# Splitting each weight block into high and low part with one instruction per engine in place of two

## The reference

```python
# first block (256 tokens)
proj = rmsnorm(x, g) @ w_in
merged = sum(sigmoid(gate_n) * (o_n @ w_branch_n) for n in range(3))
x = x + rmsnorm(merged @ w_out, g)
u = causal_depthwise_conv(rmsnorm(x, g) @ w_ffn_up, conv_w, conv_b)
x = x + rmsnorm((gelu(u_gate) * u_val) @ w_ffn_down, g)
# second block: two layers over 256 latent and 256 context tokens;
# the second layer's late part is for the latent tokens alone
m = silu(cond) @ w_mod + b_mod                      # 9 x 1024 modulation values
x = x + 0.5 * m * swiglu(modulate(rms_norm(x)), w_in, w_out)
x = x + m * mixer(attention, fourier, gates)
x = x + 0.5 * m * swiglu(...)
```

## Time and profile before

| | us |
|---|---|
| median of 3 runs (3000.58 to 3006.28) | 3004.92 |
| the profiled execution, first to last instruction | 3003.6 |
| TensorE matmul busy | 2742.5 (91%) |
| VectorE busy | 2033.8 (68%) |
| GpSimd busy | 1600.6 (53%) |
| ScalarE busy | 1054.9 (35%) |
| mean granted TensorE clock | 0.947 |

### The profile page before, as it was taken

The page is one execution under the profiler, slowest core; times in us unless marked ns, Lnnn a source line. Parts: engine busy times, 40 slices in busy tenths (PEclk is TensorE's granted clock), DMA queues, the critical chain, the costliest instruction groups (busy, mean ns, idle before and its releaser), DMA issues.

```text
span 3003.6 us, 45318 instructions
## 1 busy us (share of the span) xinstructions
PE 2742.5 (91%) x15118; PEld 2345.7 (78%) x15118; DVE 2033.8 (68%) x4077; ACT 1054.9 (35%) x1699; POOL 1600.6 (53%) x654
## 2 busy tenths in 40 slices
PE   7898878777999999988997999999999979888998
PEld 7867878776888877956786788887888868688997
DVE  4864876686887666364879888668886662656642
ACT  4344335524232132246221433214232142453542
POOL 3516836554665444335254566445665554457675
PEclk9899879987999999999998999999999989999999
DMA  5604524353443444201344344443443442035454
GB/s 175 204 22 137 172 85 140 121 153 118 154 140 118 130 143 126 64 22 57 99 126 126 112 140 135 119 137 119 147 140 111 129 138 92 22 103 164 140 169 125
DMA packets 487725, 365.71 MB, mean 122 GB/s; under 512 B 7484, under 2 KB 486286, under 8 KB 487616
## 3 DMA queue, kind: packets, MB, share of 16 engines
q1 hardware_dynamic: 485176, 359.14, 39.2%
q10 hardware_dynamic: 2440, 5.16, 0.5%
HBM read 363.19 MB, written 1.08 MB: 121 GB/s over the span
## 4 chain that ended last, share of the span: by engine, by line
PE 54%; issue 21%; POOL 12%; DVE 10%; ACT 2%; DMA 1%; POOLq 0%; DVEq 0%; SPq 0%; ACTq 0%
PE bank L1485 46%; POOL w_lo L595 12%; DVE mod_acc L1079 3%; DVE mod_acc L1075 1%; ACT work L738 1%; PE bank L1874 1%; DVE stat L1396 1%; PE bank L1495 1%; PE bank L1852 1%; PE bank L1618 1%; PE bank L1811 1%; DMA mod_raw<-in_w_mod 1%; PE bank L1861 1%; DVE root L1414 1%; PE bank L1803 0%
## 5 line engine op out<-in xcount | busy, mean ns | idle before, releaser
L595 POOL TENSOR_TENSOR w_lo<-raw,w_hi 128x1024 fp32r<-128x1024 f32 (+2 forms) x602 | 1523.5, 2546 | 1332.9 <-ACT w_hi L653 938.5
L1485 PE MATMUL bank<-u_hi,w_hi 128*128 128x512 f32 (+1 forms) x2488 | 866.8, 348 | 31.4 <-DVE work L1280 27.7
L1485 PE MATMUL bank<-u_hi,w_lo 128*128 128x512 f32 (+1 forms) x2488 | 856.9, 344 | 0.0
L1485 PE MATMUL bank<-u_lo,w_hi 128*128 128x512 f32 (+1 forms) x2488 | 856.2, 344 | 0.0
L653 ACT ACTIVATE w_hi<-raw 128x1024 fp32r<-128x1024 f32 (+3 forms) x436 | 408.9, 952 | 1080.0 <-PE bank L1485 857.5
L1079 DVE SCALAR_TENSOR_TENSOR mod_acc<-mod_raw,cond,mod_acc 128x128 f32<-128x128 f32 x2016 | 615.4, 377 | 0.0
L1485 PEld LDWEIGHTS bank<-u_hi,w_hi 128*128 128x128 f32 x2488 | 486.2, 195 | 85.5 <-DVE work L1280 29.5
L1485 PEld LDWEIGHTS bank<-u_lo,w_hi 128*128 128x128 f32 x2488 | 485.5, 195 | 52.1 <-issue 1.5
L1485 PEld LDWEIGHTS bank<-u_hi,w_lo 128*128 128x128 f32 x2488 | 484.5, 195 | 52.3
L1075 DVE TENSOR_SCALAR mod_acc<-mod_raw,cond 128x128 f32<-128x128 f32 x288 | 260.6, 944 | 117.4 <-DMA mod_raw<-in_w_mod 117.2
L1485 PE MATMUL bank<-hid_hi,w_hi 128*128 128x512 f32 (+1 forms) x880 | 314.3, 357 | 15.5 <-DVE hid_lo L1270 7.2
(11 more groups left out here) (222 smaller groups left out, 3614.5 us busy)
## 6 DMA issues: line engine op xcount, KB each, us to landing
raw<-in_ffn_w_in SPq DMA_DIRECT2D x88, 1024.0 KB, 5.1
mod_raw<-in_w_mod SPq DMA_DIRECT2D x144, 512.0 KB, 3.8
raw<-in_w_in SPq DMA_DIRECT2D x67, 1024.0 KB, 5.3
raw<-in_ffn_w_out SPq DMA_DIRECT2D x64, 704.0 KB, 4.5
raw<-in_w_ffn_up SPq DMA_DIRECT2D x22, 1024.0 KB, 5.1
raw<-in_w_ffn_down SPq DMA_DIRECT2D x16, 704.0 KB, 4.5
raw<-in_w_attn_out SPq DMA_DIRECT2D x8, 1024.0 KB, 5.0
raw<-in_w_o SPq DMA_DIRECT2D x8, 1024.0 KB, 5.0
```

Source lines behind the costliest of these rows:

```text
L595: pool.tensor_tensor(st.half(t, w_lo[slot]), st.half(t, raw[slot]), st.half(t, w_hi[slot]).bitcast(f32), ALU.subtract).then_inc(lo_ready, 1)
L1485: ins = pe.matmul(dst, s, v, start=first and n == 0, stop=final and n == 2)
```

## The change

`half` goes and `whole` takes its place. ScalarE and GpSimd issue one instruction each for the whole block. The ScalarE instruction waits for the second group of block n. `hi_ready` and `lo_ready` count blocks, so each of TensorE's waits, for the first half too, is a wait for the whole block.

```diff
-    def half(self, t, block):
-        if self.cols == P:
-            a, b = (0, DOWN_HALF) if t == 0 else (DOWN_HALF, self.kt)
-            return block[:, a * P:b * P].rearrange("p (k n) -> p k n", n=P)
-        return block[:, 0:self.kt * BLK].rearrange("p (k n) -> p k n", n=BLK)[:, :, t * P:(t + 1) * P]
+    def whole(self, block):
+        return block[:, 0:self.kt * self.cols]
...
     def parts(self, i, c, t):
-        return i * (2 * self.per) + (2 * (self.first + c) + t + 1)
+        return i * self.per + (self.first + c + 1)
...
-                    s = st.parts(i, c, 1) - 4
+                    s = st.parts(i, c, 1) - 2
...
-                    for t in range(2):
-                        pool.wait_ge(hi_ready, st.parts(i, c, t))
-                        pool.tensor_tensor(st.half(t, w_lo[slot]), st.half(t, raw[slot]), st.half(t, w_hi[slot]).bitcast(f32),
-                                           ALU.subtract).then_inc(lo_ready, 1)
+                    pool.wait_ge(hi_ready, st.parts(i, c, 1))
+                    pool.tensor_tensor(st.whole(w_lo[slot]), st.whole(raw[slot]), st.whole(w_hi[slot]).bitcast(f32),
+                                       ALU.subtract).then_inc(lo_ready, 1)
...
                 act.wait_ge(raw_ready[n % 2], i * (8 * st.per) + 16 * (n // 2 + 1))
-                for t in range(2):
-                    act.wait_ge(group_done, st.freed(i, c, t))
-                    act.activation(st.half(t, w_hi[n % 2]), st.half(t, raw[n % 2]), ACT.Copy).then_inc(hi_ready, 1)
+                act.wait_ge(group_done, st.freed(i, c, 1))
+                act.activation(st.whole(w_hi[n % 2]), st.whole(raw[n % 2]), ACT.Copy).then_inc(hi_ready, 1)
```

More of the change, by code:

```diff
@@ L634, in split @@
                 act.wait_ge(raw_ready[s % 2], 16 * (s // 2 + 1))
-                for t in range(2):
[L636 to L642, removed]
+                if s >= 2:
+                    old = [q for q in stream if q.first <= s - 2 < q.first + q.blocks][0]
+                    q = s - 2 - old.first
+                    act.wait_ge(group_done, old.freed(q // old.per, q % old.per, 1))
+                act.activation(st.whole(w_hi[s % 2]), st.whole(raw[s % 2]), ACT.Copy).then_inc(hi_ready, 1)
             def split_two_ahead(st, i, c, final):
```

## The result

The changed kernel takes 3069.15 us (median of 4 runs, 3061.49 to 3070.0), the one before 3005.6 in runs beside it: a ratio of 1.021, 95% interval 1.0194 to 1.0226. It is slower beyond doubt; whether by a full 2% the interval leaves open. The profiled execution has a span of 3066.5 us for 3003.6, so 62.9 us are to be placed. Of all executions behind this document one ran at a much lower granted clock (3153.4 us at 0.817, in experiment 11, where the others have 0.936 to 0.951), and it is left out.

A forecast was written before the change was run, and what follows sets the result against it. Wide stages were taken as bound by TensorE, up_11 as keeping TensorE busy, up1 by VectorE held by GpSimd. Terms 13 + 4 + 8 + 13 + 3 + 7 + 0 + 4 + 1 = 53 us gave 3058 us, 1.8% slower; range 3012 to 3085.

The forecast's parts named there:

- `up1`: Narrow stage: VectorE held a second time by a whole subtraction, body 17.2 us for 15.83, ten times: +13 us.
- Cost of a whole-block instruction: ScalarE's split and GpSimd's subtraction of 2048 elements take 1.90 and 4.7 us; 1408 elements take 1.37 and 3.25.
- `up_11`, the series: Narrow stage: matmuls, split and subtraction run in series, 12.8 us a round for 11.52, ten rounds: +13 us.
- `up1` opens up: Rival: TensorE's pause leaves VectorE 2.1 us in up1, no second hold, -30 for +13: 3015 us, chance 0.17.
- the state keeps itself up: Argument against a shorter up1: once VectorE is held, the later L858 pushes the split behind it.
- wide bodies: Wide stages: the series of 1.9 and 4.7 us lies under the other buffer's 10.9 us: 0.
- `gates1`: gates1_0 and gates1_1, bound by VectorE: two holds of 4.7 us replace four of 2.4: 0, within 1 us a body.
- `down_11`: Narrow stage with the load in its ring: +0.4 us for each of 8 rounds, last block later: +4 us.
- `down1`: down1, its last body bound by the ring as in down_11, and the start: together +3 us.
- Blocks of `attn_out_1` and `gates_10`: Eight narrow blocks bound as up_11 is, four rounds: +5 us.
- branches: Twelve branch blocks and four of four_out_1, bound by the load ring, plus entry of the next gemm: +7 us.
- norms: After down projections and w_o, the last subtraction ends 0.7 us later; nine places, half of them felt: +4 us.

The follow-up runs named there:

- experiment 11: Whole instructions and one step per block in gates1_0, gates1_1 and gates1_2 alone, against the kernel before: 3012.95 us, ratio 1.0028.
- Experiment 3: Kernel before with halves kept, but both halves wait for the whole block and TensorE gets one step per block, everywhere: 3030.75 us, 1.0089.
- experiment 1: Kernel before with only ScalarE's split as one instruction per block; GpSimd and TensorE keep halves: 3031.78 us, 1.0089.
- experiment 2: Kernel before with only GpSimd's subtraction as one instruction per block; ScalarE keeps halves: 3068.62 us, 1.0216.
- experiment 6: Kernel before; in up1 alone ScalarE's halves wait for the whole group, GpSimd for the whole high part, TensorE goes by halves: 3000.13 us, 0.9992.
- experiment 8: Kernel before with whole instructions and one step per block everywhere but in up1, which keeps halves: 3074.28 us, 1.0242.
- experiment 4: Kernel before with the change, one instruction each per block, in up1 alone: 2974.89 us, 0.9909.
- experiment 5: Kernel before with halves everywhere, but in up1 alone all waits are for the whole block: 2973.74 us, 0.9894.
- experiment 12: Kernel before with the change in up1 and all wide stages, halves in the narrow ones: 2983.83 us, 0.9927.

## Why the forecast came out as it did

3069 lies 11 us above the forecast and in its range, but this nearness is luck: in the traces `up1` came out 37.5 us below its term and all the rest 47.4 above theirs. By its own steps:

**Cost of a whole-block instruction: right.** ScalarE 1.91 to 1.92 us (1.90 forecast), GpSimd 4.50 to 4.65 without VectorE in its way (4.7 forecast). For 1408 elements: 1.38 and 3.19 to 3.24 (1.37 and 3.25). Some of the arithmetic was loose without moving the result: the two pieces of ScalarE's slope are 0.97 and 0.82 ns an element and not both 0.85, and the lowest bounds add up to 6.49 and not 6.45. The Trainium skill's GPSIMD Engine Reference (section "Elementwise — side-by-side cycle accounting") with its 4497 ns was nearer to the shortest, 4.50, and my line nearer to the usual 4.62.

**`up_11`, the series: right.** 12.78 us a round for 12.8 and +12.0 for +13; with the change in this stage alone +13.3. Experiment 3 shows that it is the series: +10.2 with halves.

**`up1`: wrong, in its sign too, and this is the step that failed.** The forecast put the second split of a body 8.1 to 9.6 us after the release of L858 (now L850), and so gave VectorE 0 to 1.5 us between the subtractions. The first half of the working was right: the split ends 5.3 us after that release and the subtraction 10.0 (L850 at 510.49; 515.81; 520.51). But the second split starts at 520.95, 10.46 after the release. I had taken TensorE's end from the phase that it had before, and had not let it slide with its own later start, though the sum for `up_11` did so. 0.9 us more decided between +13 and -24.5. The rival "`up1` opens up" named this mechanism, its threshold of 2.1 us and -30 us; I gave it 0.17 because "the state keeps itself up". That is right for each part alone, where the long body comes back even after a short one (experiments 1, 2 and 6), and wrong for the parts together.

**`gates_11`: not in the sum.** It has TensorE, ScalarE's sigmoid, VectorE's gate and a branch's statistics in a chain inside each block, and I had counted narrow gemms with slack in VectorE only. +14.6, by itself +12.5: one piece is the sigmoid behind a longer split, one the hold of 4.49 us for 2.36, the rest the lower clock (0.76 for 0.89) of a TensorE that now pauses. I did not separate the three. Long splits alone give +4.2, the waits alone +6.3, and long subtractions with one step for TensorE +11.2 (experiments 1, 3 and 2), so the long subtractions are probably the largest. `gates_01` has the same build: +6.4, where the forecast had 0 for wide bodies.

**`gates1`: open.** 0 forecast, +9.4 in the one execution, +0.5 to +1.5 in all others that I have (experiments 1, 2, 3, 8 and 11), but +6 in the median of experiment 11's runs.

**`down_11`: the size.** Rounds of 9.5 to 9.8 for 9.4 (loads that land 0.2 us later, after 4.7) and one late load: +8.4 for +4. **`down1`** +7.5 for +3, of which experiment 8, with `up1` in halves, shows +2.8. **First stages:** without a term of their own, +6.6 (the +3 of `down1` also speaks of "the start"); `q_me`'s +6.2 stands in experiments 2, 3 and 8 as well, not in 1, so it comes from GpSimd or TensorE waiting for a whole block. **Blocks of `attn_out_1` and `gates_10`, branches, norms, `f_1`, wide `up` and `down` bodies:** within 3 us of their terms. The +7 of the branches adds up to 5.8 from its own parts, eight rounds of 0.35 and 3; +6.2 was measured.

**The rule on breaking up instructions** (the Trainium skill, Perfetto Trace Analysis, section "Optimizing Scalar/DVE Operations") agrees with `up_11` (+12.0 without the halves) and `gates_11` (+14.6). In `up1` the opposite is measured (-24.5). What counts there is not the size of the instructions, since halves with one step per block are as fast as whole ones (experiments 4 and 5). It is the release by halves: work that completes sooner takes the time in which VectorE would have run.

What stays open besides `gates1`: why `up_00` takes 6 to 8 us less in experiments 3 and 4, and not in 5 and 12. It was not tried.

## What to carry to other kernels

When a ring of engines is closed by an edit, let every member of it slide, each stage by itself, before reading the gap that another engine gets: here 0.9 us more than forecast carried the gap over the 2.1 us that decided. Look for the gemms whose queues carry other work between the groups: the same edit costs 3 us a block in `gates_11` (12.5 in four) and 0.6 in `up_11` (13.3 in 22). And make such a change by stage: the same edit is worth -1% in `up1` alone and +2% everywhere.

## Not expected of the hardware

A delay can be worth more than the work it delays: with TensorE and ScalarE both released later, and nothing made shorter, `up1` went from 15.83 to 13.03 us a body, and TensorE's granted clock in it from 0.93 to 1.00. It now pauses for 1.19 us in a body, for the subtraction (before 514.64), where it paused for 2.6 to 2.8 us, for VectorE's L1280 (before 513.28 and 529.11). And a hold works both ways: a subtraction that takes 4.5 to 4.65 us with nothing in its way took 7.41 in `q_me`, beside VectorE's modulation products. GpSimd's timeline after, and VectorE's:

```profile
153.40 7.41 POOL L591 TENSOR_TENSOR w_lo<-raw,w_hi 128x2048 fp32r<-128x2048 f32 x1 [7.78 <-ACT w_hi L636]
```

```profile
152.68 3.76 DVE L1071 SCALAR_TENSOR_TENSOR mod_acc<-mod_raw,cond,mod_acc 128x128 f32<-128x128 f32 x14
```

VectorE had 3.0 us of its fourteen short products left when the subtraction began, and the subtraction took 2.8 us more than alone.
